# Expert rounds of a decoder step: the tokens of a round gathered as rows and turned afterwards, two spreads moved behind the gather

## The reference

```python
u = rms_norm(h, g_norm).reshape(n, d)            # 264 tokens x 1024
gates = route(u, ...)                            # (264, 16), two experts per token are not zero
a = jnp.einsum('td,edf->tef', ub, wg)            # 16 experts, 1024 -> 512
c = jnp.einsum('td,edf->tef', ub, wu)
hh = jax.nn.silu(a) * c * gb[:, :, None]
out = jnp.einsum('tef,efd->td', hh, wd)          # 512 -> 1024, summed over the experts
h = h + out
```

## Time and profile before

| | us |
|---|---|
| median of three runs | 1278.0 |
| profiled execution | 1273.8 |
| its span, first to last instruction | 1272.0 |
| PE busy in the span | 1142.9 |
| layer 0's rounds, from the first gather | 593.91 |
| layer 1's rounds, from the first gather | 975.19 |

### The profile page before, as it was taken

How to read it: one execution, slowest core, us unless ns; L and a number is a source line. 1 busy time by engine, 2 the same in 40 slices (tenths; PEclk the granted TensorE clock), 3 DMA queues, 4 the chain that set the end, 5 groups by cost and what they waited for, 6 DMA issues and landing times.

```text
span 1272.0 us, 16186 instructions
## 1 busy us (share of the span) xinstructions
PE 1142.9 (90%) x5441; PEld 736.3 (58%) x5442; DVE 428.3 (34%) x843; ACT 224.4 (18%) x508; POOL 225.1 (18%) x484
## 2 busy tenths in 40 slices
PE   5999799999949899974999999999474999999998
PEld 2887688778822688863455455554353455545554
DVE  3356456755820466123111011112733111101113
ACT  1122122122110144111111111111001111111110
POOL 1014212411410122002022222210002022222210
PEclk9999899999957699975899999999665899999999
DMA  9999999999789988899999999999999699999996
GB/s 372 332 380 379 397 387 359 342 398 386 273 291 357 395 263 292 333 364 322 329 431 429 428 398 405 417 392 389 377 335 332 263 390 392 388 390 392 399 423 229
DMA packets 62931, 462.64 MB, mean 364 GB/s; under 512 B 12112, under 2 KB 20192, under 8 KB 47888
## 3 DMA queue, kind: packets, MB, share of 16 engines
q1 hardware_dynamic: 49136, 440.29, 89.5%
q0 software_dynamic: 5536, 18.88, 4.0%
q10 hardware_dynamic: 8232, 3.13, 1.0%
HBM read 455.19 MB, written 183.41 MB: 502 GB/s over the span
## 4 chain that ended last, share of the span: by engine, by line
PE 59%; DVE 7%; issue 3%; DMA 3%; ACT 1%; POOL 1%; ACTq 1%; POOLq 0%; DVEq 0%; SPq 0%
PE bank L1228 17%; PE bank L1214 11%; PE bank L1254 8%; PE bank L1203 5%; PE bank L1165 2%; PE bank L1097 2%; DMA region_a<-in_w_up_dram 2%; PE bank L1124 1%; PE bank L1132 1%; PE bank L1144 1%; PE bank L1175 1%; PE bank L285 1%; PE bank L1260 1%; PE bank L1104 1%; PE bank L1121 1%
## 5 line engine op out<-in xcount | busy, mean ns | idle before, releaser
L1053 PE MATMUL bank<-uT,ring_lo 128*128 128x264 f32 x1152 | 273.9, 392 | 8.5 <-DVE uT L298 6.0
L1053 PEld LDWEIGHTS bank<-uT,ring_lo 128*128 128x128 f32 x1152 | 218.0, 194 | 48.8 <-issue 9.7
L1214 PE MATMUL bank<-scratch 128*128 128x128 f32 (+1 forms) x768 | 149.3, 328 | 18.0 <-POOL scratch L568 18.0
L1214 PEld LDWEIGHTS bank<-scratch 128*128 128x128 f32 (+1 forms) x768 | 113.9, 204 | 50.6 <-POOL scratch L568 18.2
L783 DVE RECIPROCAL scratch<-scratch 128x264 f32<-128x264 f32 x48 | 86.5, 1802 | 112.0 <-ACT scratch L630 112.0
L1228 PE MATMUL bank<-ring_lo,scratch 128*64 128x512 f32 x512 | 117.5, 613 | 0.0
L1254 PE MATMUL bank<-ring_lo,scratch 128*64 128x512 f32 x512 | 113.4, 595 | 0.8 <-issue 0.8
L1228 PE MATMUL bank<-region_a,scratch 128*64 128x512 f32 x512 | 112.6, 592 | 0.9 <-DMA region_a<-in_w_up_dram 0.9
L959 DVE TENSOR_TENSOR scratch<-bank,scratch 128x512 f32<-128x512 f32 x16 | 11.1, 692 | 291.6 <-PE bank L1228 291.6
L553 POOL TENSOR_TENSOR small<-epsc 128x1 f32<-128x1 f32 x83 | 16.0, 195 | 387.4 <-PE bank L1260 334.8
L1228 PEld LDWEIGHTS bank<-region_a,scratch 128*64 128x64 f32 x512 | 37.0, 137 | 73.9 <-issue 73.9
(11 more groups left out here) (220 smaller groups left out, 1206.4 us busy)
## 6 DMA issues: line engine op xcount, KB each, us to landing
out_dram<-in_cache_kv_w_dram SPq DMA_DIRECT2D x128, 1023.5 KB, 18.0
ring_lo<-in_w_gate_dram SPq DMA_DIRECT2D x32, 2048.0 KB, 12.0
region_a<-in_w_up_dram SPq DMA_DIRECT2D x32, 2048.0 KB, 15.2
ring_lo<-in_w_down_dram SPq DMA_DIRECT2D x32, 2048.0 KB, 16.1
ring_lo<-in_w_qkv_dram SPq DMA_DIRECT2D x18, 2048.0 KB, 17.0
out_dram<-in_cache_kv_w_dram SPq DMA_DIRECT2D x32, 1022.0 KB, 33.2
ring_lo<-in_cache_kv_w_dram POOLq DMA_DIRECT2D x24, 512.0 KB, 10.4
ring_lo<-in_cache_kv_w_dram SPq DMA_DIRECT2D x6, 2048.0 KB, 13.8
```

The costliest lines, as they stand in the source:

```text
L1053: last = mm(z_bank[s % 4][:, 0:T], w[:, k, at:at + P], uT[:, k, :], start=(k == 0), stop=(k == KT - 1))
L1214: last = mm(bank[m // 4][:, m % 4 * P:(m % 4 + 1) * P], u_tok[0:sizes[b], b, m * P:(m + 1) * P], pick[0:sizes[b], b, :], start=(b == 0), s ...
```

## The change

The gather has `pick` stationary and 512 features of `u_tok` moving: 2 halves by 3 token blocks instead of 8 tiles by 3 blocks. Its result has the slots on partitions, so it is copied to `u_rows` (a new piece of scratch), turned by 8 transposes into the same banks, and copied to `u_slots` as before. Spreads 0 and 1 stand between the gather and these transposes; their additions stand behind VectorE's second copy. Spreads 2 and 3 stay behind the up product, with VectorE's product waited for only ahead of spread 3.

```diff
+        u_rows = cut(8720, (D,))
...
                     ac.wait_ge(gathered, q * 2 + 4)
+                    nc.scalar.activation(u_rows[:, 512:], bank[1][:, :], ACT.Copy).then_inc(rows_act, 1)
+                    ac.wait_ge(slots_turned, q * 2 + 2)
                     nc.scalar.activation(u_slots[:, KT // 2:, :], bank[1].rearrange("p (k n) -> p k n", n=P), ACT.Copy).then_inc(slots_act, 1)
...
                 dve.wait_ge(gathered, q * 2 + 3)
+                vec.tensor_copy(u_rows[:, 0:512], bank[0][:, :]).then_inc(rows_dve, 1)
+                dve.wait_ge(slots_turned, q * 2 + 1)
                 vec.tensor_copy(u_slots[:, 0:KT // 2, :], bank[0].rearrange("p (k n) -> p k n", n=P)).then_inc(slots_dve, 1)
+                add_spread(q + layer, range(2))
                 dve.wait_ge(silu_ready, q + 1)
                 dve.wait_ge(up_done, q + 1)
                 vec.tensor_tensor(hid_rows, bank[3][:, :], silu, ALU.mult).then_inc(hid_rows_ready, 1)
-                add_spread(q + layer, 0)
+                add_spread(q + layer, range(2, 4))
                 dve.wait_ge(hid_turned, q + 1)
                 vec.tensor_copy(hid[:, 0:2, :], ...).then_inc(hid_dve, 1)
-                add_spread(q + layer, 1)
+                add_spread(q + layer, range(4, KT))
...
-                for m in range(KT):
+                for a in range(2):
                     for b in range(3):
-                        last = mm(bank[m // 4][:, m % 4 * P:(m % 4 + 1) * P], u_tok[0:sizes[b], b, m * P:(m + 1) * P],
-                                  pick[0:sizes[b], b, :], start=(b == 0), stop=(b == 2))
-                    if m % 4 == 3:
-                        last.then_inc(gathered, 1)
+                        last = mm(bank[a][:, :], pick[0:sizes[b], b, :], u_tok[0:sizes[b], b, a * 512:(a + 1) * 512],
+                                  start=(b == 0), stop=(b == 2))
+                    last.then_inc(gathered, 1)
+                pe.wait_ge(y_copied, q * 2 + 2 * (layer + 1))
+                pe.wait_ge(place_ready, q + (layer + 1))
+                for m in range(2):
+                    spread_out(m)
+                for a, rows_copied in enumerate((rows_dve, rows_act)):
+                    pe.wait_ge(rows_copied, q + 1)
+                    for m in range(4 * a, 4 * a + 4):
+                        last = nc.tensor.transpose(bank[a][:, m % 4 * P:(m % 4 + 1) * P], u_rows[:, m * P:(m + 1) * P], ident[:])
+                    last.then_inc(slots_turned, 1)
                 pe.wait_ge(slots_dve, q + 1)
...
-                pe.wait_ge(y_copied, q * 2 + 2 * (layer + 1))
-                pe.wait_ge(place_ready, q + (layer + 1))
-                for m in range(4):
-                    if m == 2:
-                        pe.wait_ge(silu_ready, q + 1)
-                        pe.wait_ge(hid_rows_ready, q + 1)
-                    spread_out(m)
+                pe.wait_ge(silu_ready, q + 1)
+                spread_out(2)
                 pe.wait_ge(hid_rows_ready, q + 1)
+                spread_out(3)
```

More of the change, by code:

```diff
@@ L250, in build @@
         gathered, slots_dve, slots_act = sem("gathered"), sem("slots_dve"), sem("slots_act")
+        rows_dve, rows_act, slots_turned = sem("rows_dve"), sem("rows_act"), sem("slots_turned")
         place_made, place_ready, y_half, y_copied = sem("place_made"), sem("place_ready"), sem("y_half"), sem("y_copied")
@@ L946, in router, with add_spread @@
                 vec.tensor_copy(rounds_i[0:1, layer * (NP + 1):(layer + 1) * (NP + 1)], rounds_f[0:1, layer, :]).then_inc(rounds_ready, 1)
-            def add_spread(n, half):
-                for m in range(4 * half, 4 * half + 4):
+            def add_spread(n, tiles):
+                for m in tiles:
                     dve.wait_ge(spread, n * KT + (m + 1))
@@ L968, in experts @@
                 end = all_of_layer(dve, layer)
-                for half in range(2):
-                    add_spread(end + layer, half)
+                add_spread(end + layer, range(KT))
                 vec.memset(small[:, 62:63], 0.0).then_inc(layer_added, 1)
```

## The result

The changed kernel took 1264.83 us in the median of four runs (1261.33 to 1266.1) against 1277.58 of the kernel before (1276.45 to 1280.06): ratio 0.9893, 95% interval 0.9868 to 0.9918. The forecast was 1261.5, in a range of 1255 to 1270. So 12.8 us are gone where 16.5 were expected. But that the total came so near is in good part luck: a steady round gains 0.46 us and not 1.21, the first round of layer 1 gains 6.4 and not 0.75, and the two errors nearly cancel in that layer.

A forecast was written before the change was run, and what follows sets the result against it. PE's own sequence was taken to bound the kernel, with transfers a near second limit. Layer 0's 6 x 1.21 = 7.3 plus layer 1's 0.75 + 7 x 1.21 = 9.2 make 16.5; 1278.0 - 16.5 = 1261.5 us, range 1255 to 1270.

The forecast's parts named there:

- The gather is then 12 x 0.427 = 5.12 us.: New gather: 12 records of 512 columns at 0.427 us each take 5.12 us, at the other end 7.10.
- 48 records in 8.44 us, 0.176 us each.: Old gather: 24 products of 128 columns are 48 records in 8.44 us, 0.176 us each.
- The head, 7.63.: From gather start to gate product: 7.63 us instead of 8.44, 0.81 gained, with 0.88 of spreads borrowed from the tail.
- The tail, 0.40 gained.: Behind the up product: two spreads fewer, transposes start at about +1.37 us instead of +1.77, 0.40 gained of 0.88.
- First rounds, 0.75 each.: Each layer's first round, gather at half clock, clock rising in the gate product as before: 0.75 us gained.
- What rounds 0 and 1 of layer 0 gain is given back.: Layer 0's start: weight landings don't move when PE is early, so the gain of 0.75 + 1.21 us is lost.
- Sum.: Whole kernel: layer 0 gains 7.3 us, layer 1 gains 9.2, together 16.5.
- Transfers did take most of layer 0's gain: Rival: weight transfers take all of layer 0's gain, 9.2 us remain, total 1268.8; chance 0.12.
- Handoffs cost nearly what the gather saves: Rival: two PE, VectorE, PE chains a round each cost 0.5 us more, 0.2 remains, total 1275; chance 0.06.
- not 0.59: Rival: wide records cost their recorded 592 ns, gather 7.10 us, each round loses 0.77, total 1290; chance 0.06.
- not 0.22: Rival: 512-column records cost half, 0.216 us, rounds 2.5 us shorter, total 1230; chance 0.02.
- The clock stayed at 1.00 in steady rounds: Rival denied here: pauses and added transposes drop the head to 1.2 GHz, near 6.6 us a round, about 1353; chance 0.02.

The follow-up runs named there:

- full-row gather: Changed kernel with the gather's 8-token block widened to 128 rows, the other 120 rows of tokens and picks zero; ratio 0.9816 to the kernel before.
- spreads-only run: Kernel before with its old gather, only spreads 0 and 1 moved from the tail to behind it; ratio 1.0076 to the kernel before.

## Why the prediction was right, and where it was not

- *"The gather is then 12 x 0.427 = 5.12 us."* This step failed. The spacing of wide records was right (0.43; the full-row gather gave 5.25), but I counted twelve of them as one row. The 8-token block cuts the row four times, and each time the next weight load starts 0.52 us behind the record before instead of together with it: 4 x 0.19 to 0.20. The gather is 5.93. The Trainium skill, "TensorE: Matmul & The Clock Gate", "The mechanism", says under "What overlaps and what doesn't" that a weight load overlaps a running product only when the row groups differ. By that neither kind of load would be hidden here, since all these blocks share the first rows; the trace differs: between blocks that use the same 128 rows the load is hidden, and only between 128 and 8 rows it is not.
- *"48 records in 8.44 us, 0.176 us each."* The average was right and hid the same cost, which I could have read before the run. The old gather changes height twice in every feature tile, 16 times in all. One tile of it, four records of 128 rows and two of 8, at full clock:

```profile
1052.47:1053.52 1.05, 1.05 (x6) 0.81 (x6) 1.00 1.05 453
```

Its records start at 1052.47, 1052.68, 1052.79, 1052.90, 1053.11 and 1053.32, the next tile's at 1053.52. Within the block of 128 rows it is 0.11 us from one to the next, at each change 0.20 to 0.21 twice: again 0.19 more per change. So of the 8.44 us some 3.1 are changes of height, and the rest is 48 x 0.111 = 5.3. Most of the 2.5 us between the old gather and the new are twelve changes fewer; the wide records alone are worth 0.2. By these numbers the old gather with its third block padded to 128 rows would take about 5.3 us and need no turn at all, a round of 31.5 us, which is just under the 31.8 at which the transfers land. That is an estimate: no run tried it.
- *The head, 7.63.* It is 8.48: 0.81 from the gather and 0.18 from PE's handoff (0.23 against the 0.05 I took from the earlier trace rows), less 0.14 because the transposes and VectorE start a little sooner behind the spreads than I put. Some 0.1 of the handoff was the waits for weights, which PE worked out only after the slot copy. The 0.49 that I expected PE to idle is 0.52.
- *The tail, 0.40 gained.* 0.51.
- *First rounds, 0.75 each.* This failed too, by a factor of nine to eleven. I kept the moment of the clock's rise where it was. It is 6.4 and 8.0. The new form of the gather is the cause: without it (spreads alone) the clock rose late, and with such products ahead of the old gather it rose early. In the kernel before and in the spreads-only run it rose 2.8 to 5.4 us into the gate product, the first of 512 columns. What in the form does it isn't shown: the old gather has narrow products and 16 changes of height, and no run puts narrow products without these changes there.
- *What rounds 0 and 1 of layer 0 gain is given back.* Right, and more: they take 81.84 us together against 80.45 (593.91 to 674.36). The second up weights land at 656.9 where they landed at 654.0; 1.5 of that is the later start of the layer; what the other 1.4 are, no run shows. From round 2 on no wait, as forecast.
- *Sum.* Layer 0 gains 1.4 instead of 7.3, layer 1 9.7 instead of 9.2 (3.2 from seven rounds, 6.4 from the first). Outside the rounds this profiled execution is 2.9 us longer (layer 0 starts 1.5 later, the stretch between the layers is 1.4 longer). The change doesn't touch these stretches, and the start of layer 0 lay between 590.5 and 595.7 in the kernels here. So 8.1 us of spans stand beside 12.8 of medians: the profiled execution before lies 3.8 below the median of its runs, the one after 1.3 above.
- *The rivals.* Transfers did take most of layer 0's gain, not by slack running out in round 2 but in round 1, whose weights were late already. "Handoffs cost nearly what the gather saves" (1.0 us a round) came nearest the size of the loss (0.75), but had it in the wrong place. The wide record costs 0.43, not 0.59 and not 0.22. The clock stayed at 1.00 in steady rounds, with twelve transposes a round instead of four.

## What to carry to other kernels

Price a row of products by its changes as well as its records: here each step between 8 and 128 rows of weights cost 0.19 to 0.20 us, and padding with zeros was cheaper than leaving rows out. Don't take an average for a pace: look at the starts of single records before pricing what is to replace them. Spend cover where the handoff is: two spreads moved in a block hid nothing in the head and bared the tail, while one before each group of transposes and two ahead of the tail's wait left PE busy through both. And when a stage gets faster, look first at the queue that feeds it; eight microseconds of layer 0 went straight into a wait for weights behind copies that nobody was waiting for.

## What the runs showed of the hardware

- Records of 128 columns with 128 rows of weights started 0.11 us apart, of 512 columns 0.43. Each change between 128 and 8 rows of weights added 0.19 to 0.20 us, in the old gather as in the new.
- PE, busy without a gap on the old gather's products of 128 columns, stayed at 1.2 GHz for all of its 15.06 us and went to 2.4 GHz 2.8 to 5.4 us into the gate product of 512 columns; with the wide gather it did so 3.3 to 9.6 us after the gather began. The moment differs from run to run: the first gather of layer 0 took 7.62 and 10.60 us in two runs of the changed kernel. During the pause of 8.0 us in round 1 it fell back to 1.2 GHz, for 6.8 us.
- Four records in a row with 8 rows of weights preceded a fall to 1.2 GHz in four of the 14 later gathers of one execution; in the changed kernel, with two in a row, none did in the 14 of either trace.
